# A hybrid decoder step on Trainium2: the FFN's down projection, 16 of 22 feature tiles as Strassen products

## The chip, the cores and the metric

One core of one Trainium2 chip runs the whole step as one program. The metric is the device time of the program in microseconds (us). For the kernel before there are three runs; their median is 1056.41 us.

## The reference, cut to what matters

One decoder layer for 512 prompt tokens and 8 sample tokens, width 1024, all in float32: token mixers, cross-attention, and last a SwiGLU feed-forward block of 2816 features.

```python
h = rms_norm(x, lp["g_ffn_pre"])
gt, up = jnp.split(h @ lp["w_gate_up"], 2, axis=-1)
f = (jax.nn.silu(gt) * up) @ lp["w_down"]
x = x + rms_norm(f, lp["g_ffn_post"])
```

`w_gate_up` is 1024 x 5632 and `w_down` is 2816 x 1024. Everything lies feature-major on the chip: a tile has 128 features on the partitions and the 520 tokens (8 sample, 512 prompt) along the free dimension. There are 8 tiles of width 1024 and 22 of 2816.

## The kernel before, in words

**Float32 by halves.** A matmul takes a value as two parts: `hi`, a rounding copy that ScalarE makes, and `lo`, the raw value less `hi`, a subtraction with two SBUF (or one PSUM and one SBUF) inputs on VectorE or GpSimd. A product of two float32 tiles is three matmuls: hi·hi, hi·lo, lo·hi. All of them move 256 to 264 token columns, one half of the 520 tokens, against a 128x128 weight.

**The front of the kernel** (input projection, RWKV scan, convolution, cross-attention) is not touched. At about 690 us the FFN's input `h` is made; its first 4 gate and 4 up tiles are done plainly (`dense`, L543, whose matmul is L556).

**Pairs as Strassen 2x2.** The other 18 gate and 18 up tiles are made in 18 units p, one gate and one up tile each (N_PAIRS = 18). The weight matrix of a unit is cut by gate/up and by first/last 4 tiles of `h`, the moving one by first/last 4 tiles and by LEFT/RIGHT 260 tokens. Seven products (`product`, L1806, matmul L1811) of 4 tiles x 3 matmuls, 84 matmuls, take the place of eight with 96. On TensorE unit p goes p6, p7, p2, p5, p1 of unit p+1, p4, p3. The four sums of operands of `h` (`t_raw`, `t_hi`, `t_lo`) are made once, ahead of the units, by operations over 1,040 columns.

**What the other engines do per unit.** VectorE, in this order (L3395 to L3510): `f_right` of the unit before (L3444), `gate_sums` (1,024 columns, two SBUF inputs, L3407), `second_sum` (L3414), `pair_f_low` of the unit before (L3448, 520 columns), `sum4_low` (L3434), `sum2_low` (L3429), y11 (L3492), `fourth_sum` (512 columns, two SBUF inputs, L3420), y22 (L3499), `sums13_low` (L3424), y21 (L3506), `f_left` (L3439). ScalarE makes the rounding copies (L2601, L2628), keeps three products (L2650, L2656, L2662), does the two silus (L2698, L2705) and `pair_f_high` (L2666). GpSimd makes three `lo` parts of 512 columns: up first half, gate second half, up second half (`pair_low`, L1055). p3 starts only when y22 has been read out of its bank, p7 of the next unit only when y21 has been used (before: by the left silu).

**The down projection** is plain: 8 output tiles m, each 22 feature tiles x 3 x 2 token halves, 132 matmuls, with weights in three blocks (8, 8 and 6 tiles, 24 blocks in all) that ScalarE (`split_hi`, L591) and GpSimd (`split_lo`, L1004) split. Six output tiles run through `dense`, the last two as pieces by token half (`down_piece`, L1878). ScalarE reads each output from PSUM twice, for its square and for the gained copy (`down_out`, L2718 and L2722), VectorE adds up the squares (`piece_add`, L3199).

**Queues.** All weight loads go through SyncE's queue in program order. `x_res`, the residual of 2,080 KB, was moved out to DRAM to make room; its return (L948) waits for the last product of the pairs, and stands between the fourth and the fifth load of down weights.

**The end.** When the first token half has all its squares, `half_sum` (L1168) and `half_root` give its norm, `half_add` (L3212, L3219) adds it to `x_res`, and `turn_tile` (L1888) transposes it for storing, while pieces of the second half fill TensorE. The last piece is followed by its squares, the root and the last transposes.

The order of work on every engine is written out by hand, with semaphores between the engines. Where two instructions of one engine follow, the later one can't pass the earlier.

## Time and profile before

| what | value |
|---|---|
| three runs, median (lowest, highest) | 1056.41 us (1055.25, 1056.93) |
| profiled execution, span of its instructions | 1055.9 us |
| TensorE busy | 1034.8 us, 98% |
| VectorE, ScalarE, GpSimd busy | 682.7, 517.8, 356.4 us |
| granted TensorE clock, mean | 0.999 |

The profile page gives no device time of its own for the profiled execution apart from the span, which lies 0.5 us under the median of the runs. The page's busy shares are means over the whole step. For this change the stretch from 735 us on counts: pairs to 916.5 us, down projection and end behind it.

### The profile page before, as it was taken

Reading aid. Unit: us, or ns where it says so; the run is one execution under the profiler, and the core shown is the slowest. Engines: PE = TensorE matmul, PEld = TensorE weight load, DVE = VectorE, ACT = ScalarE, POOL = GpSimd, SP = SyncE. Lnnn points to the kernel's source line nnn. Section 1 sums busy time; section 2 is a strip of 40 time slices with the busy share of each in tenths; the row PEclk is TensorE's granted clock in tenths of the full one; section 3 lists DMA queues with packets and bytes.
Section 4 is the critical chain, followed back from the end, with each engine's and each line's share of the span. In section 5 each row is a group of like instructions: output and inputs, shape, how many; then the busy total and the mean of one; then the engine's idle time right before and its main releaser. Section 6 shows DMA issues by size and latency. Waiting matters only on the chain.

```text
span 1055.9 us, 25943 instructions
## 1 busy us (share of the span) xinstructions
PE 1034.8 (98%) x10943; PEld 972.5 (92%) x10943; DVE 682.7 (65%) x1216; ACT 517.8 (49%) x967; POOL 356.4 (34%) x194
## 2 busy tenths in 40 slices
PE   8999999999999999999999999999999999999998
PEld 8998898998988998999999768989999999999998
DVE  5488888788785666786570791657998989500004
ACT  6455534544544567525462544654665665522232
POOL 4431221332312310256232101353544544444450
PEclk9999999999999999999999999999999999999999
DMA  7321221220223433655154774523334334433222
GB/s 228 100 70 35 61 62 43 61 76 27 62 62 102 130 102 130 209 180 164 57 200 160 259 276 131 147 76 105 110 92 120 105 97 121 161 115 100 81 64 82
DMA packets 164059, 120.41 MB, mean 114 GB/s; under 512 B 5336, under 2 KB 153066, under 8 KB 163433
## 3 DMA queue, kind: packets, MB, share of 16 engines
q1 hardware_dynamic: 159979, 108.08, 33.0%
q10 hardware_dynamic: 3974, 10.80, 2.9%
q8 instruction: 81, 1.33, 0.5%
q14 instruction: 25, 0.20, 0.1%
HBM read 111.04 MB, written 8.30 MB: 113 GB/s over the span
## 4 chain that ended last, share of the span: by engine, by line
PE 80%; DVE 13%; ACT 3%; DMA 2%; issue 2%; POOL 0%; DVEq 0%; ACTq 0%; SPq 0%
PE ps L556 34%; PE ps L1811 15%; PE ps L538 10%; PE ps L1168 10%; DVE conv_y L2859 5%; PE ps L1878 3%; PE ps L578 2%; DVE cache L3301 1%; DMA q_bc<-q_scratch 1%; PE ps L1115 1%; DVE ps L3214 1%; PE ps L604 0%; DMA w_raw<-in_w_gate_up_dram 0%; DMA x_tok<-in_x_prompt_dram 0%; DVE m_lo L640 0%
## 5 line engine op out<-in xcount | busy, mean ns | idle before, releaser
L1004 POOL TENSOR_TENSOR w_lo<-w_raw,w_hi 128x1024 fp32r<-128x1024 f32 (+2 forms) x83 | 193.7, 2338 | 408.7 <-ACT w_hi L596 356.5
L556 PE MATMUL ps<-h_hi,w_hi 128*128 128x260 f32 x748 | 161.8, 297 | 1.1 <-DVE gate_b L3156 0.5
L556 PE MATMUL ps<-h_hi,w_lo 128*128 128x260 f32 x748 | 150.2, 282 | 0.0
L556 PE MATMUL ps<-h_lo,w_hi 128*128 128x260 f32 x748 | 150.2, 282 | 0.0
L596 ACT ACTIVATE w_hi<-w_raw 128x1024 fp32r<-128x1024 f32 (+2 forms) x95 | 91.2, 965 | 74.0 <-PE ps L556 62.1
L556 PEld LDWEIGHTS ps<-h_hi,w_hi 128*128 128x128 f32 x748 | 115.3, 188 | 10.5 <-issue 4.4
L556 PEld LDWEIGHTS ps<-h_lo,w_hi 128*128 128x128 f32 x748 | 115.2, 188 | 0.0
L556 PEld LDWEIGHTS ps<-h_hi,w_lo 128*128 128x128 f32 x748 | 115.2, 188 | 0.0
L2859 DVE SCALAR_TENSOR_TENSOR conv_y<-glu,prm,conv_y 128x512 f32<-128x512 f32 x120 | 106.6, 889 | 2.5
L3199 DVE TENSOR_TENSOR sq_acc<-sq_acc,sq_tmp 128x264 f32<-128x264 f32 (+2 forms) x35 | 28.6, 816 | 114.8 <-ACT sq_tmp L2718 76.0
L1055 POOL TENSOR_TENSOR w_lo<-w_raw,w_hi 128x512 fp32r<-128x512 f32 x36 | 50.5, 1403 | 98.7 <-ACT w_hi L2601 98.7
L1168 PE MATMUL ps<-big 64*64 64x64 f32 (+1 forms) x1664 | 58.1, 232 | 5.5 <-ACT big L2053 3.6
L1004 POOL TENSOR_TENSOR wx_lo<-w_raw,wx_hi 128x1024 fp32r<-128x1024 f32 x12 | 28.7, 2394 | 101.5 <-ACT wx_hi L596 101.5
L1168 PEld LDWEIGHTS ps<-big 64*64 64x64 f32 x1664 | 48.4, 134 | 12.2 <-DVE tmp L2880 3.6
L556 PE MATMUL ps<-f_hi,w_hi 128*128 128x260 f32 x264 | 53.2, 283 | 0.3 <-DVE ps L3439 0.3
L556 PE MATMUL ps<-f_lo,w_hi 128*128 128x260 f32 x264 | 53.1, 283 | 0.0
L556 PE MATMUL ps<-f_hi,w_lo 128*128 128x260 f32 x264 | 53.1, 283 | 0.0
L556 PEld LDWEIGHTS ps<-f_hi,w_hi 128*128 128x128 f32 x264 | 40.7, 188 | 0.5 <-issue 0.5
L1811 PE MATMUL ps<-t_lo,w_hi 128*128 128x260 f32 x144 | 40.8, 283 | 0.0
L1811 PE MATMUL ps<-h_lo,w_hi 128*128 128x260 f32 x144 | 40.7, 283 | 0.0
L556 PEld LDWEIGHTS ps<-f_hi,w_lo 128*128 128x128 f32 x264 | 40.7, 188 | 0.0
L1811 PE MATMUL ps<-h_hi,w_hi 128*128 128x260 f32 x144 | 40.6, 282 | 0.0
(574 smaller groups left out, 3087.1 us busy)
## 6 DMA issues: line engine op xcount, KB each, us to landing
w_raw<-in_w_gate_up_dram SPq DMA_DIRECT2D x44, 512.0 KB, 4.7
w_raw<-in_w_in_dram SPq DMA_DIRECT2D x38, 512.0 KB, 3.7
cache<-in_cache_mem_k_dram SPq DMA_DIRECT2D x16, 512.0 KB, 6.3
w_raw<-in_w_down_dram SPq DMA_DIRECT2D x16, 512.0 KB, 3.7
cache<-in_cache_mem_v_dram SPq DMA_DIRECT2D x14, 512.0 KB, 7.3
w_raw<-in_w_k_dram SPq DMA_DIRECT2D x8, 512.0 KB, 3.9
w_raw<-in_w_v_dram SPq DMA_DIRECT2D x8, 512.0 KB, 3.6
w_raw<-in_w_out_dram SPq DMA_DIRECT2D x8, 512.0 KB, 3.7
```

Source lines behind the costliest of these rows:

```text
L538: mm = nc.tensor.matmul(ps[:, 2 * (b % 2) + h, 0:TOK_N[t][h]], w[:, k, :], x[:, k, TOK[t][h]], start=(k == 0 and n == 0), stop=(k == KT - ...
L556: mm = nc.tensor.matmul(ps[:, 2 * s + a, 0:width], w[:, k, :], x[:, x0 + k, a * width:(a + 1) * width], start=(first and k == 0 and n == 0 ...
L578: mm = nc.tensor.matmul(ps[:, 2 * a + m, :], x[:, k, P * m:P * (m + 1)], wide_rows(w)[:, kk, :], start=(k == 0 and n == 0), stop=(k == KT ...
L596: nc.scalar.activation(weights(b)[0][:, 0:kts], w_raw[:, b % RAW_SLOTS, 0:kts], ACT.Copy).then_inc(w_hi_ready, 1)
L1004: pool.tensor_tensor(lo[:, 0:kts], w_raw[:, b % RAW_SLOTS, 0:kts], hi[:, 0:kts].bitcast(F32), ALU.subtract).then_inc(w_lo_ready, 1)
L1055: pool.tensor_tensor(lo, raw, hi.bitcast(F32), ALU.subtract).then_inc(pair_lo, 1)
L1115: nc.tensor.matmul(ps[:, 2 * b + h, 0:EARLY_N[h]], hi[:, k, :], x[:, k, EARLY[h]], start=(k == 0 and n == 0), stop=False)
L1168: return nc.tensor.matmul(out, lhsT, rhs, start=start, stop=stop)
L1811: mm = nc.tensor.matmul(out, w[:, k, :], x[:, k, :], start=(start and k == 0 and n == 0), stop=(k == KT // 2 - 1 and n == 2), skip_group_c ...
L1878: mm = nc.tensor.matmul(ps[:, 2 * (m % 2) + h, 0:TOK_N[2][h]], w[:, k, :], x[:, k0 + k, TOK[2][h]], start=(j == 0 and k == 0 and n == 0), ...
L2859: link_v(stt(conv_y[:, p, 0:T], src, w, conv_y[:, p, 0:T], ALU.mult, ALU.add))
L3199: ins = tt(sq_acc[:, cols], sq_acc[:, cols], sq_tmp[:, n % 2, cols], ALU.add)
```

## The change

Eight units are put behind the 18 pairs (N_UNITS = 26). A down unit works on two output tiles (2q+1 and 2q, the place of gate and up) and on 8 of the first 16 feature tiles, as the same seven products; units 18 to 21 take feature tiles 0 to 7, units 22 to 25 tiles 8 to 15 and add to the results of 18 to 21 in `y_buf` in SBUF. The last 6 feature tiles (16 to 21) stay plain: 16 pieces of 18 matmuls, first all eight outputs of the first token half, then of the second, each added to `y_buf` by VectorE (`down_sum`).

The moving operands of the down units are parts of f named L, R, A, B, C, D (four tiles by 260 tokens, 1,040 columns): A, B, C, D are sums. f tiles 0 to 15 are now kept raw in SBUF as they come, and the sums, rounding copies and low parts of the parts are put into the loops by tables: `F_SUMS`, `F_LOWS` and their `_LATE` forms on VectorE, `F_HIGHS` on ScalarE, `FX_LOW_P` on GpSimd. Each such operation has 1,040 columns with SBUF inputs. `pair_f_high` and `pair_f_low` stay for f tiles 16 to 21 alone. In the down units f_left, f_right and the silus fall away; y11, y22, y21 go to `y_buf`, in units 22 to 25 as two operations each. The eight weight blocks of the last 6 feature tiles get storage of their own, seven of them in the room of used f parts. The return of `x_res` waits for the last product of all 26 units and again stands between the fourth and fifth load of the remaining blocks.

The diff, cut to its core:

```diff
-PAIR_BLOCKS = 2 * N_PAIRS
-N_BLOCKS = B_DOWN + 3 * KT
-DOWN_KT = (8, 8, 6)
+N_DOWN = 8
+N_UNITS = N_PAIRS + N_DOWN
+PAIR_BLOCKS = 2 * N_UNITS
+N_BLOCKS = B_DOWN + KT
+REST = 2 * KT
+REST_KT = FT - REST
...
+        if B_DOWN <= b < B_DOWN + 5:
+            return wd_a[:, b - B_DOWN], wd_b[:, b - B_DOWN]
+        if B_DOWN + 5 <= b < B_DOWN + 7:
+            return wd_b[:, b - B_DOWN], wd_b[:, b - B_DOWN + 2]
+        if b == B_DOWN + 7:
+            return w_hi[:, 0], w_lo[:, 0]
...
+    FX_HI = ("L0", "A0", "L1", "B0", "C0", "D0", "R1", "L2", "L3", "A2", "B2", "C2", "R3", "D2")
+    FX_LOW_V = ("L0", "B0", "C0", "L1", "A0", "D0", "C2", "B2", "D2")
+    FX_LOW_P = ("R1", "L2", "A2", "L3", "R3")
+    FX_RAW = ("A0", "B0", "C0", "D0", "A2", "B2", "C2", "D2")
...
+    FX_AT = {"L0": (rows(f_hi, 0, LEFT), rows(f_lo, 0, LEFT), rows(f_raw, 0, LEFT)),
+             "R0": (None, None, rows(f_raw, 0, RIGHT)),
+             "B0": (rows(f_hi, 0, RIGHT), rows(f_lo, 0, RIGHT), rows(f_raw, 0, RIGHT)),
+             "L1": (rows(f_hi, 1, LEFT), rows(f_lo, 1, LEFT), rows(f_raw, 1, LEFT)),
+             "R1": (rows(t_lo, 1, RIGHT), rows(f_lo, 1, RIGHT), rows(f_raw, 1, RIGHT)),
+             "A0": (rows(f_lo, 2, RIGHT), rows(f_lo, 2, LEFT), rows(f_raw, 2, LEFT)),
+             "C0": (rows(f_lo, 3, RIGHT), rows(f_lo, 3, LEFT), rows(f_raw, 3, LEFT)),
+             "D0": (rows(t_lo, 0, RIGHT), rows(f_hi, 1, RIGHT), rows(fh_raw, 1, RIGHT)),
+             "L2": (rows(h_hi, 0, LEFT), rows(f_hi, 2, LEFT), rows(fh_raw, 2, LEFT)),
+             "R2": (None, None, rows(fh_raw, 2, RIGHT)),
+             "B2": (rows(h_hi, 1, RIGHT), rows(f_hi, 2, RIGHT), rows(fh_raw, 2, RIGHT)),
+             "L3": (rows(t_lo, 1, LEFT), rows(f_hi, 3, LEFT), rows(fh_raw, 3, LEFT)),
+             "R3": (rows(t_lo, 0, LEFT), rows(f_hi, 3, RIGHT), rows(fh_raw, 3, RIGHT)),
+             "A2": (rows(h_hi, 1, LEFT), rows(h_lo, 0, LEFT), rows(hl_raw, 0, LEFT)),
+             "C2": (rows(h_lo, 1, RIGHT), rows(h_lo, 1, LEFT), rows(hl_raw, 1, LEFT)),
+             "D2": (rows(t_lo, 0, RIGHT), None, None)}
+    D2_LOW = (two(dx_low_a[:, :]), two(dx_low_b[:, :]))
+    D2_RAW = (two(rs[:, :]), two(silu[:, :]))
...
+    def f_operand(p, name):
+        g = 2 * ((p - N_PAIRS) // 4)
+        n = {"p1": f"L{g}", "p2": f"L{g + 1}", "p3": f"R{g + 1}", "p4": f"D{g}", "p5": f"A{g}", "p6": f"C{g}",
+             "p7": f"B{g}"}[name]
+        return n
...
+    def down_bank(m, h):
+        return (1, 3, 7, 1, 3, 7, 3, 1)[m] if h else (0, 2)[m % 2]
...
+            for m in range(KT):
+                src = weight_view("w_down")[:, REST:FT, P * m:P * (m + 1)]
+                if m < RAW_SLOTS:
+                    at = (B_DOWN + m) % RAW_SLOTS
+                    if m % 2 == 0:
+                        pair_slots_free(N_UNITS + m // 2)
+                    sp.dma_start(w_raw[:, at, 0:REST_KT], src).then_inc(w_landed[at], 16)
                 else:
-                    load(B_DOWN + n, src, kts=kts)
-                if n == RAW_SLOTS - 1:
+                    load(B_DOWN + m, src, kts=REST_KT)
+                if m == RAW_SLOTS - 1:
                     sp.wait_ge(product_done, PRODUCTS)
                     sp.wait_ge(x_moved, 16)
                     sp.dma_start(x_res[:, :, :].rearrange("p k n -> p (k n)"), x_scratch).then_inc(x_moved, 16)
...
+            def f_part_low(n):
+                hi, lo, raw = FX_AT[n]
+                pool.wait_ge(f_hi_ready, f_high(n))
+                pool.wait_ge(f_sums_made, f_summed({"R1": "D0", "L2": "A2", "A2": "C2", "L3": "D2", "R3": "D2"}[n]))
+                pool.tensor_tensor(lo, raw, hi.bitcast(F32), ALU.subtract).then_inc(f_low_p, 1)
+            for p in range(N_UNITS):
+                if p + 1 < N_UNITS:
                     pair_low(p + 1, "p1", pair_raw(p + 1)[2], "ua")
                 pair_low(p, "p4", pair_raw(p)[1], "gb")
-                if p + 1 < N_PAIRS:
+                if p == N_PAIRS:
+                    f_part_low("R1")
+                if p + 1 < N_UNITS:
                     pair_low(p + 1, "p2", pair_raw(p + 1)[3], "ub")
+                if N_PAIRS + 1 <= p < N_PAIRS + 5:
+                    f_part_low(FX_LOW_P[p - N_PAIRS])
...
+                if p in (N_PAIRS, N_PAIRS + 4):
+                    pe.wait_ge(*f_low(f_operand(p, name)))
...
+            def down_piece(m, h):
+                b = B_DOWN + m
                 hi, lo = weights(b)
                 pe.wait_ge(w_lo_ready, b + 1)
-                if j == 0 and h == 0:
-                    pe.wait_ge(out_taken[m % 2], (B_DOWN + m) // 2)
-                k0 = sum(DOWN_KT[:j])
-                for k in range(DOWN_KT[j]):
+                if h == 0 and m < 2:
+                    pe.wait_ge(f_made, fs(N_UNITS - 2 + m, 2))
+                elif h == 0:
+                    pe.wait_ge(down_summed, down_sums(m - 2, 0))
+                elif m < 2:
+                    pe.wait_ge(y_made, ys(N_UNITS - 1, ("y11", "y21")[m]))
+                elif m > 2:
+                    pe.wait_ge(down_summed, down_sums(m - 2 if m == 6 else m - 3, 1))
+                for k in range(REST_KT):
                     for n, (w, x) in enumerate(((hi, f_hi), (hi, f_lo), (lo, f_hi))):
-                        mm = nc.tensor.matmul(ps[:, 2 * (m % 2) + h, 0:TOK_N[2][h]], w[:, k, :], x[:, k0 + k, TOK[2][h]],
-                                              start=(j == 0 and k == 0 and n == 0),
-                                              stop=(j == 2 and k == DOWN_KT[2] - 1 and n == 2))
-                if j == 2:
-                    mm.then_inc(block_done if h else a_done, 1)
+                        mm = nc.tensor.matmul(ps[:, down_bank(m, h), 0:TOK_N[2][h]], w[:, k, :], x[:, REST + k, TOK[2][h]],
+                                              start=(k == 0 and n == 0), stop=(k == REST_KT - 1 and n == 2))
+                mm.then_inc(block_done if h else a_done, 1)
...
+            for m in range(KT):
+                down_piece(m, 0)
+            down_piece(0, 1)
             half_sum(2, 0)
-            down_piece(KT - 2, 1, 1)
-            down_piece(KT - 2, 2, 1)
-            down_piece(KT - 1, 0, 1)
-            pe.wait_ge(a_taken, A_TAKEN + 2)
+            for m in range(1, 5):
+                down_piece(m, 1)
+            pe.wait_ge(a_taken, A_TAKEN + KT)
             turn_tile(0, (0, 2), ready=KT * 4)
...
+            F_HIGHS = {1: ("L0",), 2: ("A0",), 5: ("L1",), 6: ("B0",), 7: ("C0",), 18: ("D0",), 19: ("L3",), 20: ("A2", "B2"),
+                       21: ("C2",), 22: ("D2",)}
+            F_HIGHS_LATE = {18: ("R1", "L2"), 21: ("R3",)}
+            def copy_up_right(p):
+                act.wait_ge(product_done, done(p, "p3"))
+                go(out_rows(p)[0][:, RIGHT], chain_bank(p), ACT.Copy).then_inc(f_made, 1)
...
+                if SPLIT_FROM < p <= N_PAIRS:
                     pair_f_high(p - 1)
+                if N_PAIRS < p <= N_PAIRS + 4:
+                    copy_up_right(p - 1)
+                for n in F_HIGHS.get(p, ()):
+                    f_part_high(n)
                 sum4_high(p)
                 keep_seventh(p)
+                for n in F_HIGHS_LATE.get(p, ()):
+                    f_part_high(n)
                 if more:
...
+                act.wait_ge(down_summed, down_sums(m, h))
...
+                rows = y_buf[:, m, TOK[2][h]]
+                go(sq_tmp[:, n % 2, TOK[2][h]], rows, ACT.Square).then_inc(post_squares, 1)
+                go(rows, rows, ACT.Copy, scale=prm_col("g_ffn_post", m)).then_inc(out_taken[m % 2] if h else a_taken, 1)
+            for b in range(B_DOWN + 2, B_DOWN + 4):
                 split_hi(b)
-            down_out(KT - 2, 0)
-            down_out(KT - 1, 0)
+            for m in range(KT):
+                if m == 3:
+                    act.wait_ge(product_done, PRODUCTS)
+                if m < 4:
+                    split_hi(B_DOWN + 4 + m)
+                down_out(m, 0)
+            down_out(0, 1)
             half_root(4)
...
+            def f_part_sum(n):
+                g = int(n[1])
+                raw = {m: FX_AT[m + str(i)][2] for m, i in (("L", g), ("R", g))}
+                left, right = FX_AT[f"L{g + 1}"][2], FX_AT[f"R{g + 1}"][2]
+                if n[0] == "A":
+                    if g:
+                        dve.wait_ge(product_done, done(N_PAIRS - 1, "p3"))
+                        dve.wait_ge(f_made, fs(REST - 5, 2))
+                    else:
+                        dve.wait_ge(out_taken[1], B_UP // 2 + 4)
+                    tt(FX_AT[n][2], raw["L"], raw["R"], ALU.subtract).then_inc(f_sums_made, 1)
+                    return
+                if n == "B0":
+                    dve.wait_ge(f_made, fs(KT - 5, 2))
+                dve.wait_ge(f_sums_made, f_summed(n) - 1)
+                if n[0] == "B":
+                    tt(FX_AT[n][2], raw["R"], right, ALU.subtract).then_inc(f_sums_made, 1)
+                elif n[0] == "C":
+                    stt(FX_AT[n][2], FX_AT[f"A{g}"][2], -1.0, right, ALU.mult, ALU.subtract).then_inc(f_sums_made, 1)
+                elif n == "D0":
+                    tt(FX_AT[n][2], left, FX_AT["C0"][2], ALU.add).then_inc(f_sums_made, 1)
+                else:
+                    for r in range(2):
+                        ins = tt(D2_RAW[r], left[:, 2 * r:2 * r + 2], FX_AT["C2"][2][:, 2 * r:2 * r + 2], ALU.add)
+                    ins.then_inc(f_sums_made, 1)
+            def f_part_low(n):
+                hi, lo, raw = FX_AT[n]
+                dve.wait_ge(f_hi_ready, f_high(n))
+                if n == "D2":
+                    for r in range(2):
+                        ins = tt(D2_LOW[r], D2_RAW[r], hi[:, 2 * r:2 * r + 2].bitcast(F32), ALU.subtract)
+                else:
+                    ins = tt(lo, raw, hi.bitcast(F32), ALU.subtract)
+                ins.then_inc(f_lo_ready, 1)
+            F_SUMS = {1: "A0", 4: "B0", 5: "C0", 6: "D0", 19: "A2", 20: "C2"}
+            F_SUMS_LATE = {19: "B2", 20: "D2"}
+            F_LOWS = {2: "L0", 7: "B0", 8: "C0", 9: "L1", 10: "A0", 18: "D0", 21: "C2", 22: "D2"}
+            F_LOWS_LATE = {21: "B2"}
...
+            def down_y(p, n):
+                up, gate = out_rows(p)
+                dst, bank, kept_part, op = {"y11": (up[:, LEFT], y11_bank, p1_kept_t[:, :], ALU.add),
+                                            "y22": (gate[:, RIGHT], chain_bank(p), p7_kept_t[:, :], ALU.subtract),
+                                            "y21": (gate[:, LEFT], y21_bank, n2_kept_t[:, :], ALU.subtract)}[n]
+                a, b = (kept_part, bank) if n == "y22" else (bank, kept_part)
+                if p < N_PAIRS + 4:
+                    tt(dst, a, b, op).then_inc(y_made, 1)
+                else:
+                    link_v(tt(kept_part, a, b, op))
+                    tt(dst, dst, kept_part, ALU.add).then_inc(y_made, 1)
+            def down_up_right(p):
+                dve.wait_ge(product_done, done(p, "p3"))
+                dst = out_rows(p)[0][:, RIGHT]
+                dve.wait_ge(f_made, fs(p - 4, 2))
+                tt(dst, dst, chain_bank(p), ALU.add).then_inc(f_made, 1)
+            for p in range(N_UNITS):
+                more = p + 1 < N_UNITS
+                if 0 < p <= N_PAIRS:
                     f_right(p - 1)
+                elif p > N_PAIRS + 4:
+                    down_up_right(p - 1)
                 if more:
                     gate_sums(p + 1)
                     second_sum(p + 1)
-                if p:
+                if SPLIT_FROM < p <= N_PAIRS:
                     pair_f_low(p - 1)
+                if p in F_SUMS:
+                    f_part_sum(F_SUMS[p])
+                if p in F_LOWS:
+                    f_part_low(F_LOWS[p])
...
+                if p in F_SUMS_LATE:
+                    f_part_sum(F_SUMS_LATE[p])
+                if p in F_LOWS_LATE:
+                    f_part_low(F_LOWS_LATE[p])
                 dve.wait_ge(product_done, done(p, "p4"))
                 dve.wait_ge(kept, keeps(p, "n2"))
-                tt(y21_bank, y21_bank, n2_kept_t[:, :], ALU.subtract).then_inc(y_made, 1)
-                f_left(p)
-                if p == 0:
-                    f_low(3)
-            f_right(N_PAIRS - 1)
-            pair_f_low(N_PAIRS - 1)
...
+            def down_sum(m, h):
+                dve.wait_ge(*((block_done, B_DOWN + m + 1) if h else (a_done, A_DONE + m + 1)))
+                if m == 0 and h == 0:
+                    dve.wait_ge(y_made, ys(N_UNITS - 1, "y21"))
+                    dve.wait_ge(f_made, fs(N_UNITS - 1, 2))
+                rows = y_buf[:, m, TOK[2][h]]
+                tt(rows, rows, ps[:, down_bank(m, h), 0:TOK_N[2][h]], ALU.add).then_inc(down_summed, 1)
+            for m in range(KT):
+                down_sum(m, 0)
+                if m:
+                    piece_add(2, m - 1, 0)
+            piece_add(2, KT - 1, 0)
+            down_sum(0, 1)
+            dve.wait_ge(a_taken, A_TAKEN + KT)
             dve.wait_ge(x_moved, 32)
-            half_add(4, range(KT), None)
-            piece_add(2, KT - 2, 1)
+            for m in range(4):
+                half_add(4, range(2 * m, 2 * m + 2), None)
+                down_sum(m + 1, 1)
+                piece_add(2, m, 1)
             dve.wait_ge(w_lo_ready, N_BLOCKS)
             dve.wait_ge(y_turns, 2)
             for d in range(2):
                 V.tensor_copy(y_tok(1)[:, 4 * P * d:4 * P * (d + 1)], ps[:, 4 + d, :]).then_inc(y_turn_v, 1)
```

## Rows read from the trace of the kernel before

**Rows 1.** The page, busy time of each engine (us, share, instructions).
```profile
PE 1034.8 (98%) x10943; PEld 972.5 (92%) x10943; DVE 682.7 (65%) x1216; ACT 517.8 (49%) x967; POOL 356.4 (34%) x194
```

**Rows 2.** Windows: window, length, busy us of PE, PEld, DVE, ACT, POOL; clock, DMA, GB/s.
```profile
800.00:900.00 100.00, 100.00 (x838) 100.00 (x837) 91.00 (x120) 60.52 (x120) 47.61 (x31) 1.00 0.36 106
...
950.00:1000.00 50.00, 50.00 (x419) 50.00 (x419) 2.38 (x4) 13.21 (x17) 21.22 (x10) 1.00 0.32 94
```

**Rows 3.** Timeline (start, us, instruction), TensorE, first matmul of two following pairs.
```profile
837.48 0.28 PE L1811 MATMUL ps<-t_hi,h_hi 128*128 128x260 f32 x1
...
847.54 0.28 PE L1811 MATMUL ps<-t_hi,h_hi 128*128 128x260 f32 x1
```

**Rows 4.** Timeline, VectorE, through one pair.
```profile
842.87 1.65 DVE L3420 TENSOR_TENSOR sum_tmp<-sum_tmp,w_raw 128x512 f32<-128x512 f32 x1
844.45 0.42 DVE L3499 TENSOR_TENSOR ps<-p_kept_t,ps 128x260 f32<-128x260 f32 x1
844.79 1.21 DVE L3424 TENSOR_TENSOR w_lo<-ps,w_hi 128x1024 fp32r<-128x1024 f32 x1
846.31 0.44 DVE L3506 TENSOR_TENSOR ps<-ps,n_kept_t 128x260 f32<-128x260 f32 x1 [0.32 <-PE ps L1811]
847.20 0.44 DVE L3439 TENSOR_TENSOR ps<-ps,silu 128x260 f32<-128x260 f32 x1 [0.45 <-ACT silu L2705]
...
848.09 2.05 DVE L3407 TENSOR_TENSOR ps<-w_raw 128x1024 f32<-128x1024 f32 x1
...
851.39 0.68 DVE L3434 TENSOR_TENSOR h_lo<-sum_tmp,h_hi 128x512 fp32r<-128x512 f32 x1
851.99 0.69 DVE L3429 TENSOR_TENSOR h_lo<-sum_tmp,h_hi 128x512 fp32r<-128x512 f32 x1
852.59 0.43 DVE L3492 TENSOR_TENSOR ps<-ps,p_kept_t 128x260 f32<-128x260 f32 x1
```

**Rows 5.** Timeline, GpSimd, the same pair.
```profile
842.69 1.29 POOL L1055 TENSOR_TENSOR w_lo<-w_raw,w_hi 128x512 fp32r<-128x512 f32 x1 [1.45 <-ACT w_hi L2601]
847.77 1.29 POOL L1055 TENSOR_TENSOR w_lo<-w_raw,w_hi 128x512 fp32r<-128x512 f32 x1 [3.79 <-ACT w_hi L2601]
849.01 2.28 POOL L1055 TENSOR_TENSOR zg_lo<-w_raw,zg_hi 128x512 fp32r<-128x512 f32 x1
```

**Rows 6.** Timeline, ScalarE, the same pair.
```profile
841.99 0.63 ACT L2601 ACTIVATE w_hi<-w_raw 128x512 fp32r<-128x512 f32 x1 [0.51 <-PE ps L1811]
...
846.78 0.39 ACT L2705 ACTIVATE silu<-ps 128x260 f32<-128x260 f32 x1 [1.21 <-DVE ps L3506]
847.07 0.62 ACT L2601 ACTIVATE w_hi<-w_raw 128x512 fp32r<-128x512 f32 x1
```

**Rows 7.** Timeline, operations of 1,024 to 1,040 columns between SBUF tiles, ahead of the pairs.
```profile
721.49 1.24 DVE L3461 TENSOR_TENSOR t_raw<-t_raw 128x1040 f32<-128x1040 f32 x1
...
721.21 3.95 ACT L2597 ACTIVATE t_hi<-t_raw 128x1040 fp32r<-128x1040 f32 x4
...
713.32 2.40 POOL L1004 TENSOR_TENSOR w_lo<-w_raw,w_hi 128x1024 fp32r<-128x1024 f32 x1
```

**Rows 8.** Timeline of SyncE behind the last product; DMA issues there, with time to landing.
```profile
916.71 0.34 SPq L948 DMA_DIRECT2D x_res<-x_scratch  x1
...
w_raw<-in_w_down_dram SPq DMA_DIRECT2D x1, 512.0 KB, 8.8
```

**Rows 9.** Timeline, ScalarE and GpSimd, the halves of one six-tile weight block.
```profile
1002.29 0.85 ACT L596 ACTIVATE w_hi<-w_raw 128x768 fp32r<-128x768 f32 x1 [3.67 <-PE ps L556]
...
1003.21 1.85 POOL L1004 TENSOR_TENSOR w_lo<-w_raw,w_hi 128x768 fp32r<-128x768 f32 x1 [2.12 <-ACT w_hi L596]
```

**Rows 10.** Timeline, TensorE and VectorE, around the first norm half of the end.
```profile
1030.96 0.61 PE L1168 MATMUL ps<-sq_acc,model_mean 128*128 128x264 f32 x2
...
1039.22 1.04 PE L1888 MATMUL ps<-ident,x_res 128*128 128x128 f32 x8
...
1038.04 0.42 DVE L3199 TENSOR_TENSOR sq_acc<-sq_acc,sq_tmp 128x256 f32<-128x256 f32 x1
```

276 lines of the change are left out of this document (147 added, 129 removed).

## The prediction, made before the changed kernel ran

> **What bounds the kernel now.** I read the page first: TensorE is busy 1034.8 of 1055.9 us [rows 1]. Then the windows from the pairs on [rows 2]: in the pairs TensorE is busy 100.00 of 100 us with VectorE at 91.00 and GpSimd at 47.61; in the down projection TensorE is full again and VectorE has 2.38 of 50 us. So matmuls set the time in both, but with very different cover: a pair has hardly 1 us of free VectorE, the plain down projection has nearly all of it. Last I read one pair engine by engine [rows 3 to 6], to find how late each result is. A change that takes matmuls out of the idle-VectorE stretch and turns that stretch into something like pairs saves TensorE time and spends VectorE's.
>
> **What goes.** The plain down projection has 8 x 132 = 1,056 matmuls. After: 8 units x 84 = 672, and 16 pieces x 18 = 288, in all 960. A pair lasts 847.54 - 837.48 = 10.06 us for 84 matmuls [rows 3], 0.1198 us each. 96 x 0.1198 = **-11.5 us**. The weight traffic is the same (8 units x 2 blocks of 512 KB, then 8 of 384 KB, for 16 and 8 before). ScalarE's reads of outputs in PSUM become reads in SBUF behind an addition on VectorE; in the 16 pieces that costs VectorE two operations of about 0.4 us in 2.16 us, beside TensorE. These are covered.
>
> **The lock between VectorE and GpSimd.** `fourth_sum` reads two SBUF tiles, has 512 columns as `sum4_low` has, and takes 1.65 us where that takes 0.68 [rows 4]: it begins at 842.87, GpSimd runs 842.69 to 843.98 [rows 5], and 843.98 + 0.54 is where it ends. `gate_sums` takes 2.05: GpSimd runs to 849.06, then 1.08 us. And GpSimd's next takes 2.28 for 1.29, since `gate_sums` held it up to 850.14. So such operations exclude each other whole, and whoever waits gets the next turn. The Trainium skill (SBUF — State Buffer, Who interferes with whom) says that the first to start holds the pair and the other fully blocks, which this agrees with; the same page gives about 115 ns more at a handover, and by that figure the forecast would be some 4 us later (five handovers a unit in seven units). The rows show 1.15 us of run behind a handover, under the 1.29 of a free one, so I add nothing.
>
> **Units 1 to 10.** `pair_f_low`, which reads PSUM and is free of the lock, falls away here; in units 1, 2 and 4 to 10 an operation of 1,040 columns with two SBUF inputs stands in its place, 1.24 us [rows 7], spacing 1.16. y22 ends at 844.87 [rows 4], TensorE wants it for p3 at 837.48 + 6 x 1.437 = 846.10: 1.2 us of slack. The first such unit uses it up: the operation waits for GpSimd until 851.29 (0.5), takes 1.1 instead of 0.6, and pushes `sum2_low` behind GpSimd's third low part (released by the copy at p2's end, 4.5 us into a unit [rows 6]), 1.2 more; `fourth_sum` then finds the lock free, 1.0 back. When the next unit is one too, everything hangs in a ring from one y22's end to the next: sums13_low 1.13, y21 0.44, silu 0.43, copy of up's first half 0.91, GpSimd 1.33, gate_sums 1.08, GpSimd 1.15, the new operation 1.10, GpSimd 1.15, sum4_low 0.54, sum2_low 0.61, y11 0.33, fourth_sum 0.61, y22 0.42, less 0.5 of overlapped starts: 10.7 us where the pace is 10.06. That is 0.62 per unit in units 5 to 10, 3.7, and 0.4 in unit 2: **+4.1 us**. Bounds: 0, if the third low part comes late enough to fall behind `fourth_sum`; 8, if both low parts and the sums collide each time.
>
> **Units 18 to 22.** Here the silus, f_left and f_right are gone (0.44 each on VectorE), but nearly all the operations on parts come together. Each is counted by what p3 or p7 waits for.
> - Unit 18: ScalarE does D0, R1 and L2 (0.99 each, [rows 7]) ahead of the copy that `sum2_low` needs, which ends 6.9 us into the unit; GpSimd's R1 low (2.4, [rows 7]) holds the lock to 8.0, sum2_low 0.54, GpSimd's waiting low part 1.15, fourth_sum 0.54, y22 0.4: 10.6 against 8.6. +2.0.
> - Unit 19: A2's sum, without f_right and silus: 0. Unit 20: C2's sum and two more copies of 0.99: y22 about 0.3 late. +0.3.
> - Unit 21: D2's sum (two halves) stands before y21 of unit 20, behind GpSimd's A2 low of 2.4: from y22's end, A2 low until 2.05, half 0.54, GpSimd 1.15, half 0.54, y21 0.4, in all 4.7; p7 is due at 2.9. +1.8.
> - Unit 22: y21 of unit 21 behind L3 low and B2 low, by the same count 3.5 against 2.9: +0.6. Then from y21's end a chain of lock turns: GpSimd 1.15, gate_sums 1.1, GpSimd 1.15, D2 low in halves 1.2, GpSimd 1.15, sum4_low 0.54, R3 low 2.4, sum2_low 0.55, y11 in two operations 0.8, fourth_sum 0.6, y22 in two 0.85: 11.5, which puts y22 at 13.6 in a unit where p3 is due at 9.4: +4.2.
> - Units 23 to 25 have the doubled adds but no parts: VectorE's 7.4 us and some 2 of lock fit: 0.
>
> Together **+8.9 us**. Bounds: 2 (only unit 18's ScalarE queue counts, the rest falls between) and 14 (each further collision another 1.2 in five units).
>
> **The last 6 tiles.** `x_res` goes out 0.2 us behind the last product; the fifth weight block stands behind it on SyncE's queue, and the one there now lands 8.8 us after its issue at 917.1 [rows 8]. Before, its place in the order was (132 + 48) x 0.1198 = 21.6 us on; now the fifth piece is due 4 x 18 x 0.1198 = 8.6 us after the last product. It lands at about 9.1 (384 KB for 512), then 0.85 on ScalarE and 1.85 on GpSimd [rows 9]: ready at 11.9. +3.3. Behind the blocked ScalarE the first square waits, behind that `piece_add` on VectorE and the next `down_sum`, which frees a bank; `piece_add` has two SBUF inputs and meets GpSimd's splits: +0.7. Between the half's `half_sum` and its transposes TensorE had 8.26 us of filler, and VectorE was done 1.2 us early [rows 10]; now VectorE has four `down_sum` and `piece_add` in between (3 us) against 8.6 us of filler: +0.5. The last piece's square has a `down_sum` and its release (0.42 + 0.2) in front: +0.6. **+5.1 us**, bounds 3 and 7.
>
> **The sum.** -11.5 + 4.1 + 8.9 + 5.1 = +6.6. The trace's span is 1055.9 us, 0.5 under the median of the three runs; I put the sum on the median: **1063.0 us**. A measurement of this kernel can tell about 0.2%, 2.1 us, from no change.
>
> **The rivals.**
> - *Likeliest, 0.59: the lock ring and the crowded units cost more than the matmuls give.* 1063.0, own range 1058.6 to 1071. For it: 91 of 100 us of VectorE and rows that show the lock. Against: the counts of units 20 to 22 build on each other.
> - *Faster, 0.31: the collisions mostly fall into gaps.* The new operations meet the lock free, as `sum4_low` does now; units 1 to 10 cost 0, the crowded ones 2, the end stays 5.1: -4.4, 1052.0. For it: the total of lock holders in such a unit is 7.7 of 10.06 us. It decides from where the stalls in the units are under 11.5 - 5.1 - 2.1 = 4.3. With the end hidden too, 1047.
> - *Even, 0.10: the two cancel*, stalls of 4.3 to 8.5 us in the units: 1056.4.
> - That the change doesn't do what it says would show as a count of matmuls other than 96 fewer; the loops in the diff leave no room for that, and I give it no chance of its own.
>
> The range: 1049 leaves out the case with the end hidden and part of the faster one, about 1 in 10; 1070 leaves out the upper bounds taken together, another 1 in 10. Chances: faster by over 0.2% 0.31, within 0.10, slower 0.59.
>
> **What the profile after would show.** 96 fewer TensorE instructions. Units 5 to 10 spaced 10.7 us instead of 10.06, with TensorE idle before p3, released by VectorE's y22; `fourth_sum` at 0.7 and `sum2_low` at 1.8 us there. Gaps before p3 of units 18 and 22 and before p7 of 21. A gap of about 3 us before the fifth piece, released by GpSimd's split of a block that landed late. Wrong: pairs still at 10.06 with the new operations in (the ring is looser than counted), or the fifth block ready in time.

## The result, and the profile after

The changed kernel takes **1069.46 us** (median of 4) against 1056.66 us of the kernel before on the same chip: ratio **1.0122**, 95% interval 1.0106 to 1.0138. That is 12.8 us slower, and the forecast 1063.0 us is 6.3 above the same median: the loss is twice the one forecast. All ratios compare runs in the faster of two states, and the medians of c5_later and c6_fill count one slower run each. The profiled execution has a span of 1067.1 us, 11.2 more than before.

The page after, to be set beside [rows 1]:

```profile
PE 1032.0 (97%) x10847; PEld 967.7 (91%) x10847; DVE 785.1 (74%) x1329; ACT 548.4 (51%) x1038; POOL 372.2 (35%) x207
```

TensorE has 96 instructions fewer (10,847 for 10,943), as the change says, and VectorE 113 more. But its busy time fell only by 2.8 us, where 96 matmuls are 11.5: some of the others must have become longer, by 8.7 us together. That is the first sign of what the forecast lacks.

The front of the kernel is the same in both, but in the two profiled executions it didn't last equally long. TensorE's first matmul of the pairs, before and then after:

```profile
735.07 0.28 PE L1811 MATMUL ps<-h_hi,w_hi 128*128 128x260 f32 x1
```

```profile
732.75 0.28 PE L1924 MATMUL ps<-h_hi,w_hi 128*128 128x260 f32 x1
```

So the front was 2.3 us shorter in the second, by chance, and from there to the end it is 320.8 us before and 334.3 us after: **+13.5 us**, and not 11.2, is what this pair of traces has to explain. Below, "from the pairs on" is reckoned in this way.

Whom TensorE waited for, from the pairs on (producer, total us, times, longest one). Before, the same view of that stretch has a single line of 0.3 us.

```profile
PE ps L1924 <- DVE y_buf L3661: 4.7, 2, 3.5
PE ps L1992 <- DVE y_buf L3728: 4.5, 1, 4.5
PE ps L1924 <- DVE ps L3701: 4.1, 8, 1.2
PE ps L1924 <- issue: 1.8, 1, 1.8
PE ps L1924 <- DVE y_buf L3658: 1.3, 1, 1.3
PE ps L1278 <- ACT sq_tmp L2853: 0.4, 1, 0.4
```

L3701 is y22 of a pair, L3658 and L3661 are single and doubled additions of a down unit, L3728 is `down_sum`. The long ones, in the timeline of TensorE (start, length, instruction, in brackets the idle time before it and who ended it):

```profile
754.20 0.36 PE L1924 MATMUL ps<-h_hi 128*128 128x260 f32 x1 [1.17 <-DVE ps L3701]
...
932.20 0.35 PE L1924 MATMUL ps<-t_lo,h_hi 128*128 128x260 f32 x1 [1.85 <-issue]
958.33 0.36 PE L1924 MATMUL ps<-f_hi,w_hi 128*128 128x260 f32 x1 [1.34 <-DVE y_buf L3658]
979.62 0.35 PE L1924 MATMUL ps<-t_lo,h_hi 128*128 128x260 f32 x1 [3.49 <-DVE y_buf L3661]
1011.37 0.36 PE L1924 MATMUL ps<-t_lo,h_hi 128*128 128x260 f32 x1 [1.16 <-DVE y_buf L3661]
1026.25 0.56 PE L1992 MATMUL ps<-f_hi,wd_a 128*128 128x264 f32 x1 [4.48 <-DVE y_buf L3728]
```

The bracket is the time in which no matmul runs. A matmul lasts 0.28 us and the next one otherwise begins 0.12 us after it, so a stall puts off all that follows by 0.16 us more than its bracket.

In order: unit 2's p3 (the first of eight such, 4.1 us together), unit 18's p3, unit 21's p7, unit 22's p3, unit 25's p3 and the third piece of the last tiles. All but unit 25's were forecast, the last one for the fifth piece. The waits add up to 16.8 us in 14 stalls, where before has three of 0.5 us together (two of them too short for that view), and the 0.16 of eleven more stalls makes 1.8. With the 11.5 us that went, that makes +6.6, and the traces have +13.5. **Some 7 us are in no wait.** Most of them are in the clock. Windows (start:end, length, busy us and instructions of PE, PEld, DVE, ACT, POOL; granted clock, DMA share, GB/s) around four of the stalls:

```profile
925.00:935.00 10.00, 8.15 (x59) 7.98 (x58) 8.93 (x10) 6.25 (x11) 7.17 (x5) 0.88 0.37 107
935.00:945.00 10.00, 10.00 (x82) 10.00 (x81) 8.04 (x10) 6.08 (x11) 4.55 (x3) 0.95 0.36 105
955.00:965.00 10.00, 8.65 (x72) 8.48 (x71) 9.97 (x11) 6.72 (x13) 6.20 (x5) 1.00 0.37 107
975.00:985.00 10.00, 6.51 (x42) 6.33 (x41) 9.26 (x12) 2.13 (x5) 4.48 (x3) 0.83 0.33 98
1025.00:1035.00 10.00, 8.75 (x52) 8.78 (x53) 6.61 (x9) 5.57 (x13) 6.41 (x4) 0.67 0.01 3
```

A full window of 10 us shows 84 to 86 matmuls. Behind unit 18's stall and behind unit 22's, TensorE is busy 8.15 and 6.51 us but issues 59 and 42 matmuls where 68 and 54 would fit; at the third piece 52 in 8.75 us. The granted clock is 0.88, 0.83 and 0.67 there. Microsecond by microsecond it is 0.50 (the 1.2 GHz level) from 933 to 936, from 981 to 983 and from 1025 to 1031, and 1.00 on either side of the first two. Behind unit 21's stall of 1.34 us it stays at 1.00. What was lost can be read from the windows: 10 us at 0.88 and 10 at 0.95 lack 1.7 us of full clock, 10 at 0.83 another 1.7, and the last window 3.3, of which 0.6 fell into the stall itself. Together that is **6.1 us** (0.8 us stay unexplained). The profiled execution is no odd one: the mean granted clock of the four runs is 0.991 to 0.995, against 0.999 before.

### The profile page after: what moved, and what is told of

Same layout as the page of the kernel before. It is cut to its first block, busy times and chain, and to the rows that moved or that the text cites. A ratio compares the mean times of both kernels' runs of the same rounds, so it can differ in the third digit from the quotient of the medians.

```text
span 1067.1 us, 26110 instructions
## 1 busy us (share of the span) xinstructions
PE 1032.0 (97%) x10847; PEld 967.7 (91%) x10847; DVE 785.1 (74%) x1329; ACT 548.4 (51%) x1038; POOL 372.2 (35%) x207
## 3 DMA queue, kind: packets, MB, share of 16 engines
q8 instruction: 84, 1.38, 0.5%
## 4 chain that ended last, share of the span: by engine, by line
PE 70%; DVE 20%; issue 4%; ACT 3%; DMA 2%; DVEq 0%; POOL 0%; ACTq 0%; SPq 0%; POOLq 0%
PE ps L570 25%; PE ps L1924 15%; PE ps L1278 10%; PE ps L552 10%; DVE conv_y L2989 4%; PE ps L1992 3%; PE ps L592 2%; DVE ps L3532 2%; DVE h_lo L3559 1%; DVE w_lo L3549 1%; DVE cache L3431 1%; DMA w_raw<-in_w_down_dram 1%; PE ps L1225 1%; DVE ps L3344 1%; DVE sum_tmp L3545 1%
## 5 line engine op out<-in xcount | busy, mean ns | idle before, releaser
L1103 POOL TENSOR_TENSOR w_lo<-w_raw,w_hi 128x1024 fp32r<-128x1024 f32 (+1 forms) x64 | 151.4, 2370 | 351.5 <-ACT w_hi L610 299.3
L570 PE MATMUL ps<-h_hi,w_hi 128*128 128x260 f32 x748 | 161.9, 298 | 0.8 <-DVE gate_b L3286 0.5
L570 PE MATMUL ps<-h_hi,w_lo 128*128 128x260 f32 x748 | 150.4, 282 | 0.0
L570 PE MATMUL ps<-h_lo,w_hi 128*128 128x260 f32 x748 | 150.4, 283 | 0.0
L1154 POOL TENSOR_TENSOR w_lo<-w_raw,w_hi 128x512 fp32r<-128x512 f32 x52 | 74.5, 1434 | 141.1 <-ACT w_hi L2709 141.1
L610 ACT ACTIVATE w_hi<-w_raw 128x1024 fp32r<-128x1024 f32 (+1 forms) x76 | 72.5, 958 | 25.9 <-PE ps L570 14.7
L1154 POOL TENSOR_TENSOR zg_lo<-w_raw,zg_hi 128x512 fp32r<-128x512 f32 x26 | 54.1, 2080 | 2.9 <-ACT zg_hi L2709 2.9
L1924 PE MATMUL ps<-h_hi,w_hi 128*128 128x260 f32 x192 | 54.4, 283 | 0.1
L1924 PE MATMUL ps<-h_hi,w_lo 128*128 128x260 f32 x192 | 54.2, 282 | 0.0
L3532 DVE TENSOR_TENSOR ps<-w_raw 128x1024 f32<-128x1024 f32 x26 | 51.5, 1981 | 0.0
L1924 PE MATMUL ps<-h_lo,w_hi 128*128 128x260 f32 x160 | 45.3, 283 | 0.0
L1924 PE MATMUL ps<-t_hi,w_lo 128*128 128x260 f32 x144 | 40.5, 282 | 0.0
L1924 PE MATMUL ps<-t_hi,w_hi 128*128 128x260 f32 x144 | 40.5, 281 | 0.0
```

The lines of the kernel that those rows point to most:

```text
L570: mm = nc.tensor.matmul(ps[:, 2 * s + a, 0:width], w[:, k, :], x[:, x0 + k, a * width:(a + 1) * width], start=(first and k == 0 and n == 0 ...
L610: nc.scalar.activation(weights(b)[0][:, 0:kts], w_raw[:, b % RAW_SLOTS, 0:kts], ACT.Copy).then_inc(w_hi_ready, 1)
L1103: pool.tensor_tensor(lo[:, 0:kts], w_raw[:, b % RAW_SLOTS, 0:kts], hi[:, 0:kts].bitcast(F32), ALU.subtract).then_inc(w_lo_ready, 1)
L1154: pool.tensor_tensor(lo, raw, hi.bitcast(F32), ALU.subtract).then_inc(pair_lo, 1)
L1924: mm = nc.tensor.matmul(out, w[:, k, :], x, start=(start and k == 0 and n == 0), stop=(k == KT // 2 - 1 and n == 2), skip_group_check=not ...
L3532: tt(sum_banks, two(others), quad(gate_a).unsqueeze(1).to_broadcast([P, 2, 4 * P]), ALU.add).then_inc(sums_made, 1)
```

## The experiments

**The slow clock by itself.** In `before`, three pairs get a hold of known length: ScalarE copies that rewrite two tiles of f_hi, which the results overwrite later, and p3 waits for them. Run d1_hold:

```diff
+    HOLD = {4: 2, 9: 3, 14: 5}
...
                 pe.wait_ge(y_made, ys(p, "y22"))
+                if p in HOLD:
+                    pe.wait_ge(held, list(HOLD).index(p) + 1)
                 product("p3", chain_bank(p), False)
...
+                if p in HOLD:
+                    for i in range(HOLD[p] - 1):
+                        link_a(go(f_hi[:, 20:22], h_hi[:, 0:2].bitcast(F32), ACT.Copy))
+                    go(f_hi[:, 20:22], h_hi[:, 0:2].bitcast(F32), ACT.Copy).then_inc(held, 1)
```

> The kernel before with three holds put in: in pairs 4, 9 and 14 TensorE waits before p3 for 2, 3 and 5 extra copies of 1,040 columns on ScalarE; results are unchanged. Expected stalls 1.3, 2.3 and 4.4 us. Theory (the clock falls behind a long enough stall): granted clock 1.00 behind the first, 0.5 for about 3.7 us behind the second and third, which costs about 1.9 us each: 8.0 of stalls and 3.8 of clock, 1068 us. Rival (stalls alone, the clock of the changed kernel fell for another reason): 1064.4 and a granted clock of 1.00 throughout.

Measured: 1068.57 us (one run), stalls of 1.23, 2.33 and 4.54 us, sum 8.1; +12.8 us from the pairs on (the span has only +10.7, since the front was 2.1 us shorter than in the trace of before). Run d2_hold is the same with other lengths:

> The kernel before, with TensorE held ahead of p3 in pairs 4, 14 and 9 by ScalarE copies that change nothing, sized between the earlier three holds: expected stalls about 1.8, 2.1 and 3.4 us (earlier 1.23, 2.33 and 4.54). Theory (behind a stall above some 2 us the clock falls, and the slow stretch has about one length, 3.5 to 4 us, however long the stall was): 1.00 behind the first, a fall behind the other two, span 1055.9 + 7.3 + 1.5 to 3.5 = 1065 to 1067. Rival (the loss grows with the stall): the 3.4 us hold loses more than half as much again as the 2.1 us one.

Measured: 1068.51 us (one run), stalls of 2.19, 3.44 and 2.12 us, sum 7.75; +12.6 from the pairs on. Windows behind the stalls of 1.23, 2.33 and 4.54, long enough to hold the whole slow stretch (d1_hold):

```profile
785.00:791.00 6.00, 5.92 (x49) 5.96 (x50) 4.57 (x7) 3.98 (x9) 3.54 (x2) 1.00 0.01 2
837.96:843.00 5.04, 5.04 (x29) 5.04 (x30) 2.94 (x4) 1.96 (x6) 2.51 (x2) 0.66 0.04 10
894.58:901.00 6.42, 6.42 (x33) 6.42 (x34) 2.91 (x4) 2.45 (x7) 2.52 (x2) 0.58 0.19 50
```

and behind 2.19, 3.44 and 2.12 (d2_hold):

```profile
786.00:791.00 5.00, 5.00 (x29) 5.00 (x30) 2.60 (x4) 1.91 (x6) 2.52 (x2) 0.66 0.02 5
841.52:849.00 7.48, 7.48 (x39) 7.48 (x40) 3.90 (x6) 3.14 (x8) 2.52 (x2) 0.59 0.34 99
896.95:903.00 6.05, 6.05 (x50) 6.05 (x51) 4.70 (x7) 3.94 (x10) 3.53 (x2) 1.00 0.02 4
```

Behind 1.23 and, in the other kernel, behind 2.12 the clock is 1.00 and some 50 matmuls fit into 6 us. Behind the other four the window lacks its length times what the clock lacks of 1.00: 1.7 us behind 2.33, 2.7 behind 4.54, 1.7 behind 2.19 and 3.1 behind 3.44. So a stall costs its own length, and a long one a slow stretch on top; for stalls near 2 us it can go either way, and the spread over all runs stands in the last section. The times bear the price out: from the pairs on, 12.8 - 8.1 - 0.5 (three times 0.16) leaves 4.2 us in d1_hold for slow stretches that lack 4.4, and 12.6 - 7.75 - 0.5 leaves 4.3 in d2_hold for 4.8. The rival of d2_hold (the loss grows with the stall) is half borne out: 3.1 behind 3.44 is well over one and a half times the 1.7 behind 2.19, but behind 4.54 it is only 2.7.

**The same in the changed kernel.** If the clock falls because TensorE stands still, matmuls that nothing reads must keep it up without ending any wait sooner. They take y11's bank, which is free until the next unit's p2. Run a6_fill:

```diff
+            def fill(n, bank):
+                for i in range(n):
+                    nc.tensor.matmul(bank, f_hi[:, REST, 0:P], f_hi[:, REST + 1, 0:HALF], start=True, stop=True)
...
                 product(p, "p4", y21_bank, False)
+                if p in (18, 22):
+                    pe.wait_ge(y_made, ys(p, "y11"))
+                    fill(13 if p == 18 else 27, y11_bank)
...
+                if m == 2:
+                    pe.wait_ge(y_made, ys(N_UNITS - 1, "y11"))
+                    fill(34, y11_bank)
                 down_piece(m, 0)
```

> The changed kernel, with matmuls that nothing reads put into its three longest stalls of TensorE: 13 ahead of p3 in unit 18 (stall 1.85 us), 27 ahead of p3 in unit 22 (3.49 us) and 34 ahead of the third piece of the last tiles (4.48 us), at 0.12 us each 1.56, 3.24 and 4.08 us, so that each ends before what TensorE waits for there. They take y11's bank, which is free by then. Nothing else is touched, and each wait ends when it did. Theory (the clock is lost because TensorE stood still): the granted clock stays 1.00 behind all three, the stalls show as 0.3 to 0.4 us each, and the 5 to 6 us that the sum of stalls and removed matmuls leaves open are gone: span 1061 to 1062.5, time 1063 to 1065. Rival 1 (the matmuls behind these places are slow because of what runs beside them on the other engines): still half speed there, time 1069 to 1070. Rival 2 (the stalls themselves are the whole price and the rest is scattered): 1069 to 1070 with the clock at 1.00.

Measured: 1067.80 us, ratio 1.0116 (1.0100 to 1.0132). The clock is 1.00 behind all three, but the time is above the 1063 to 1065 expected: a miss, with a plain cause in the trace. In unit 22 y11's addition had ended only 2.04 us into the stall, the 27 matmuls began then, and they ran on 2 us past y22. By its interval this run can't be told from the changed kernel. Run a7_fill cuts them to 11:

> The changed kernel with the unread matmuls of the run a6_fill, the 27 of unit 22 cut to 11. In a6_fill they could only start when y11's double addition was done, 2.04 us into the stall, and at 3.3 us they ran on past the end of the wait by some 2 us (y22 had landed at 978.91, they ended at 981.07); 11 take 1.3 us and end about when y22 lands. Theory (the clock is lost because TensorE stands still, and those 2 us of overrun are why a6_fill was only 1.7 us below the changed kernel): clock 1.00 behind all three stalls, span of the profiled execution 1061.5 to 1063, median time 1063.5 to 1066 (changed kernel 1069.5). Rival (a kept clock is worth 2 us at most): 1067 or more.

Measured: **1064.74 us**, ratio 1.0073 (1.0055 to 1.0091), span 1061.5. Waits and windows of a7_fill:

```profile
PE ps L1924 <- DVE ps L3711: 4.1, 8, 1.2
PE ps L1953 <- DVE y_buf L3671: 2.0, 1, 2.0
PE ps L1924 <- DVE y_buf L3668: 1.4, 1, 1.4
PE ps L1924 <- DVE y_buf L3671: 1.2, 1, 1.2
```

```profile
925.00:935.00 10.00, 9.85 (x81) 9.56 (x80) 8.94 (x11) 6.57 (x11) 7.79 (x5) 1.00 0.36 107
935.00:945.00 10.00, 10.00 (x86) 10.00 (x85) 9.45 (x12) 6.08 (x11) 5.59 (x3) 1.00 0.36 107
975.00:985.00 10.00, 7.96 (x65) 7.82 (x65) 9.71 (x15) 3.60 (x8) 3.46 (x3) 1.00 0.33 96
1025.00:1035.00 10.00, 10.00 (x84) 9.94 (x83) 6.49 (x11) 4.27 (x12) 3.11 (x2) 1.00 0.01 2
```

Clock 1.00 in every window where it was 0.88 to 0.67. Waits (9.1) and filler (58 x 0.12 = 7.0) together are 16.1 us, hardly less than the changed kernel's waits of 16.8 in the same stretch, and yet the median is 4.7 us lower, and the trace from the pairs on 6.0. So this is the term that no wait shows: **4 to 5.5 us for the clock**, where the windows of the changed kernel lack 6.1, and the rival (2 us at most) falls.

**The last tiles.** Run a1_xres_last sends the read of `x_res` behind all weight blocks on SyncE's queue, nothing else:

```diff
-                if m == RAW_SLOTS - 1:
+                if m == KT - 1:
                     sp.wait_ge(product_done, PRODUCTS)
```

> The changed kernel with one edit: the return of x_res is issued behind all eight remaining weight blocks instead of behind the fourth. Theory (a stall costs its own length and then some us of matmuls at half the clock): the gap of 4.48 us before the third piece goes and with it the stretch of 90 matmuls that took 13.49 instead of 10.78 us, together 7.2: 1069.5 to 1062.3 us. Rival 1 (only the wait counts, the slow clock has another cause): the gap goes, the slow stretch stays, 1065.0. Rival 2 (GpSimd's splits or the sums on VectorE bound the pieces anyway): under 2 us of gain, 1067.5 or more.

Measured: 1062.42 us, ratio 1.0057 (1.0040 to 1.0074): 7.0 us gained by one line, more than the stall of 4.5 that it removes, since the slow stretch goes with it (85 matmuls from 1025 to 1035 for 52). Part of the 7.0 isn't its own: unit 18's stall is there with 1.86 us, but in this execution no slow stretch followed it. The chain that it cuts, in the changed kernel (SyncE's issues, ScalarE's and GpSimd's splits, VectorE):

```profile
1013.09 0.34 SPq L1047 DMA_DIRECT2D x_res<-x_scratch  x1
1013.47 8.67 SPq L902 DMA_DIRECT2D w_raw<-in_w_down_dram  x4
1022.88 0.84 ACT L610 ACTIVATE wd_a<-w_raw 128x768 fp32r<-128x768 f32 x1 [12.22 <-DMA w_raw<-in_w_down_dram]
1023.80 1.80 POOL L1103 TENSOR_TENSOR wd_b<-w_raw,wd_a 128x768 fp32r<-128x768 f32 x1 [8.90 <-ACT wd_a L610]
1024.07 1.69 DVE L3326 COPY sq_acc<-sq_tmp 128x264 f32<-128x264 f32 x1 [6.20 <-ACT sq_tmp L2853]
1025.68 0.42 DVE L3728 TENSOR_TENSOR y_buf<-y_buf,ps 128x264 f32<-128x264 f32 x1
```

The block's issue at 1013.47 stands behind `x_res`, it lands 9.4 us later (8.8 in [rows 8], for a larger block), ScalarE's first half goes at 1022.88, the square that had queued behind it at 1023.63, and then `piece_add` takes 1.69 us: it ends at 1025.76, and GpSimd's split of the same block, begun before it, ends at 1025.60. This first `piece_add` is a copy with one SBUF input, so here too VectorE stood for GpSimd, though the operation hasn't the two inputs of which the forecast spoke. Only then comes `down_sum`, which frees the third piece's bank. The stall came at the third piece and not at the fifth, 4.48 us long for a forecast of 3.3 + 0.7.

**Units 1 to 10.** Run a2_parts_late moves their nine part operations behind `sums13_low`:

```diff
-            F_SUMS = {1: "A0", 4: "B0", 5: "C0", 6: "D0", 19: "A2", 20: "C2"}
-            F_SUMS_LATE = {19: "B2", 20: "D2"}
-            F_LOWS = {2: "L0", 7: "B0", 8: "C0", 9: "L1", 10: "A0", 18: "D0", 21: "C2", 22: "D2"}
-            F_LOWS_LATE = {21: "B2"}
+            F_SUMS = {19: "A2", 20: "C2"}
+            F_SUMS_LATE = {1: "A0", 4: "B0", 5: "C0", 6: "D0", 19: "B2", 20: "D2"}
+            F_LOWS = {18: "D0", 21: "C2", 22: "D2"}
+            F_LOWS_LATE = {2: "L0", 7: "B0", 8: "C0", 9: "L1", 10: "A0", 21: "B2"}
```

> The changed kernel with one edit: the nine operations of 1,040 columns of units 1 to 10 stand behind sums13_low instead of ahead of sum4_low, with the same work. Theory (the ring of turns at the lock with GpSimd): there the lock is free, p3 no longer waits for y22, and the eight stalls of 4.1 us in all fall under 1: 1066 us or less. Rival (VectorE has simply too much work in these units, wherever it stands): the stalls move to another product and stay at 3 to 4 us, 1069.

Measured: 1063.97 us, ratio 1.0063 (1.0046 to 1.0080); the eight stalls are gone from the waits, the others stand as they did (4.7, 4.5, 1.9 and 1.4). The median gained 5.5, the traces from the pairs on differ by 3.7: between them lie the 4.1 of the waits. The rival (the stalls move to another product) falls.

**Unit 18: ScalarE's queue or the lock?** The forecast's count has both: three copies on ScalarE, behind which the one that `sum2_low` needs ends 6.9 us into the unit, and GpSimd's R1 low, which holds the lock to 8.0. Run a3_unit18 takes one of them (L2's) to unit 19:

```diff
-F_HIGHS = {..., 19: ("L3",), ...}
-F_HIGHS_LATE = {18: ("R1", "L2"), 21: ("R3",)}
+F_HIGHS = {..., 19: ("L2", "L3"), ...}
+F_HIGHS_LATE = {18: ("R1",), 21: ("R3",)}
```

> The changed kernel with one edit: ScalarE's rounding copy of L2 goes from unit 18 to unit 19. Theory of the prediction (the queue of copies on ScalarE ahead of the one that sum2_low needs makes the stall of 1.85 us in unit 18): the stall falls to about 0.9 and the clock behind it stays at 1.00, 2.5 us in all, 1067. Rival (the turns at the lock alone make it, GpSimd's R1 low and the low part behind it): the stall stays at 1.85, and the time within 1 us of 1069.5.

Measured: 1072.16 us (one run); `sum2_low` begins earlier, but the stall stays at 1.84, and a new one of 2.18 stands at 957.22, where L2's copy now is in the way. Run c2_free joins this with the two remedies above and lets the second operations read and write banks free of the lock, as the next fence shows for y22:

```diff
-                    link_v(tt(kept_part, a, b, op))
-                    tt(dst, dst, kept_part, ALU.add).then_inc(y_made, 1)
+                    room = f_banks[:, 1] if n == "y22" else bank
+                    link_v(tt(room, a, b, op))
+                    tt(dst, dst, room, ALU.add).then_inc(y_made, 1)
```

> Both edits, and two more: ScalarE's copy of L2 goes from unit 18 to unit 19, and the second operation of y11, y22 and y21 in units 22 to 25 reads its first input from PSUM, so that it has no two SBUF inputs and needs no lock. Theory: against the changed kernel -7.2 (x_res), -3.5 (units 2 to 10), -2.9 (unit 18: stall from 1.85 to about 0.9 and no slow stretch behind it), -1.2 (unit 25), -0.8 (unit 22): 1054 us, a little under the kernel before. Rival (collisions only move): 1060 or more.

Measured: 1058.89 us, ratio 1.0019 (1.0006 to 1.0032), between the theory and its rival; the stall of unit 25 is gone, 1.85 still stand in unit 18 and 3.5 in unit 22, and 2.15 in unit 20, to which L2's copy moved. VectorE in unit 18 of the changed kernel (`gate_sums`, `sum2_low`, y22), then the same of c2_free with GpSimd's R1 low as its last line:

```profile
922.10 2.05 DVE L3532 TENSOR_TENSOR ps<-w_raw 128x1024 f32<-128x1024 f32 x1
928.31 1.78 DVE L3554 TENSOR_TENSOR h_lo<-sum_tmp,h_hi 128x512 fp32r<-128x512 f32 x1 [1.07 <-ACT h_hi L2709]
931.69 0.41 DVE L3658 TENSOR_TENSOR y_buf<-p_kept_t,ps 128x260 f32<-128x260 f32 x1
```

```profile
919.47 2.07 DVE L3532 TENSOR_TENSOR ps<-w_raw 128x1024 f32<-128x1024 f32 x1
924.72 2.74 DVE L3554 TENSOR_TENSOR h_lo<-sum_tmp,h_hi 128x512 fp32r<-128x512 f32 x1
929.07 0.41 DVE L3658 TENSOR_TENSOR y_buf<-p_kept_t,ps 128x260 f32<-128x260 f32 x1
924.25 2.66 POOL L1163 TENSOR_TENSOR f_lo<-f_raw,t_lo 128x1040 fp32r<-128x1040 f32 x1 [1.56 <-ACT t_lo L2802]
```

From `gate_sums` to y22 it is 931.69 - 922.10 = 9.59 us and 929.07 - 919.47 = 9.60. Without the ScalarE copy `sum2_low` (L3554) has no wait for it any more (1.07 before), but it meets GpSimd's R1 low and takes 2.74 us instead of 1.78. So L2's copy is not in the path of y22, and R1's low on GpSimd is. ScalarE isn't out of it altogether: R1's low itself waited 1.56 us for ScalarE's copy of R1 (last line), ahead of which D0's copy stands, and no run moved those two.

**Order in units 18 to 25.** Run a4_y22_first puts y11 and y22 ahead of `sum2_low` and `fourth_sum`, and the late part operations behind y21, in the down units only:

```diff
-                if more:
+                if more and p < N_PAIRS:
                     sum2_low(p + 1)
...
-                if more and p:
+                if more and p and p < N_PAIRS:
                     fourth_sum(p + 1)
...
+                if more and p >= N_PAIRS:
+                    sum2_low(p + 1)
+                    fourth_sum(p + 1)
                 if more:
                     sums13_low(p + 1)
```

> The changed kernel with one edit: in the down units VectorE takes y11 and y22 ahead of sum2_low and fourth_sum, and the late part operations behind y21, with the same work. Theory (p3 waits for a reader that needs no lock but stands in the queue behind two that do): stall of unit 18 from 1.85 to 0.3, of unit 21 from 1.34 to 0.3, of unit 22 from 3.5 to 0.8 (R3 low itself on GpSimd), and no slow clock behind any of them: 5.3 of stalls and about 4 of clock less, 1060.5 us. Rival (the lock has too little time in these units in whatever order): the stalls go to p6 and p7 of the next units, 1066 or more.

Measured: 1067.65 us, ratio 1.0111 (1.0085 to 1.0138): the rival. Unit 18's stall went, but 3.37 us (unit 22's p7 waits for B2's low), 0.70 and 2.04 us now stand in unit 22; the stalls from 733 us on add up to 17.8 us, for 16.8. That the time isn't longer has its cause in the clock: only the last of these stalls has a slow stretch behind it. Run c3_order joins the remedies of a1, a2 and the free banks with this order:

> The changed kernel with four edits: x_res behind all weight blocks, the parts of units 1 to 10 late, the lock-free second operations, and the order of VectorE in the down units (L2's copy stays in unit 18). By the sum of the single runs: 1069.5 - 7.1 (x_res, measured) - 5.5 (parts late, measured) - 1.2 (unit 25) - 9 (order) = 1046.7 us, about 1% under the kernel before. Rival (what is won in one unit is paid in the next): 1053 or more.

Measured: 1056.05 us, ratio 0.9997 (0.9983 to 1.0010): the time of the kernel before, and again the rival's. The order has gained something here: c2_free, which lacks it (and has L2's copy in unit 19), took 1058.89. Where it stalls, and a window of it:

```profile
951.92 0.36 PE L1924 MATMUL ps<-f_hi,w_hi 128*128 128x260 f32 x1 [1.38 <-DVE y_buf L3658]
965.60 0.36 PE L1924 MATMUL ps<-h_hi,w_hi 128*128 128x260 f32 x1 [3.40 <-DVE f_hi L3642]
```

```profile
943.00:967.00 24.00, 19.23 (x158) 18.87 (x158) 23.90 (x25) 13.86 (x26) 14.80 (x8) 1.00 0.33 96
```

From 943 to 967 VectorE is busy 23.90 of 24 us, against 91.00 of 100 in a pair [rows 2]. From one `gate_sums` to the next it takes 11.7 us (942.04, 953.76, 965.38), where TensorE's unit takes 10.06: VectorE has more work, with its waits for the lock, than fits. Run c5_later tests whether another place for the lock's holders helps. It takes GpSimd's L2 and A2 lows away from the fourth sums:

```diff
-                if p == N_PAIRS:
-                    f_part_low("R1")
+                if p in (N_PAIRS, N_PAIRS + 2, N_PAIRS + 3):
+                    f_part_low({N_PAIRS: "R1", N_PAIRS + 2: "L2", N_PAIRS + 3: "A2"}[p])
...
-                if N_PAIRS + 1 <= p < N_PAIRS + 5:
+                if N_PAIRS + 3 <= p < N_PAIRS + 5:
                     f_part_low(FX_LOW_P[p - N_PAIRS])
```

> The version with four remedies (x_res behind the last block, parts of units 1 to 10 late, lock-free second operations, y22 ahead of the sums in the down units; 1056.05), and on top GpSimd's part lows L2 and A2 put behind the next unit's p4 low, so that they no longer stand where VectorE makes the fourth sum (2.92 us there instead of 1.66). Theory (in units 19 to 21 VectorE is busy without a gap from 921 to 969 us, so it is the amount of work under the shared lock that counts, and a turn saved at one operation is taken at another): stalls of TensorE between 942 and 967 still add up to 4 to 5 us, time 1055 to 1057. Rival (the place of GpSimd's operations is what costs): the fourth sums fall to 1.7 us, stalls fall by about 2.4 us, time 1052 to 1053.5.

Measured: 1057.66 us, ratio 1.0012 (1.0001 to 1.0024), a little above the 1055 to 1057 expected and far from the rival's 1052 to 1053.5. VectorE in the same halves of D2's sum and the same fourth sum, c3_order, then c5_later:

```profile
947.36 2.94 DVE L3545 TENSOR_TENSOR sum_tmp<-sum_tmp,w_raw 128x512 f32<-128x512 f32 x1
953.15 0.69 DVE L3631 TENSOR_TENSOR silu<-fh_raw,hl_raw 128x520 f32<-128x520 f32 x1
```

```profile
948.16 0.68 DVE L3545 TENSOR_TENSOR sum_tmp<-sum_tmp,w_raw 128x512 f32<-128x512 f32 x1
951.72 2.94 DVE L3631 TENSOR_TENSOR silu<-fh_raw,hl_raw 128x520 f32<-128x520 f32 x1
```

The fourth sum fell from 2.94 to 0.68, as wished, and the half of D2's sum rose from 0.69 to 2.94: GpSimd's A2 low (951.20 to 954.11) now stands there. Stalls between 942 and 967: 0.99 + 4.21 = 5.2, against 1.38 + 3.40 = 4.8. Moving these two lows gained nothing, which is what the theory says: the amount of work under the lock counts, not its place.

**A version that beats both.** What can still be had in c3_order is the clock behind its 3.40 us. Run c6_fill adds 26 unread matmuls there:

```diff
                 product(p, "p6", chain_bank(p), False)
+                if p == 22:
+                    pe.wait_ge(y_made, ys(p - 1, "y11"))
+                    fill(26, y11_bank)
```

> The same version (1056.05), with 26 matmuls that nothing reads ahead of p7 in unit 22, where TensorE stands 3.40 us for B2's low and then runs about 3.3 us at half speed. Theory of the clock: no slow stretch, stall down to 0.3 us, 1.6 to 1.8 us gained: time 1054.0 to 1054.8, below the kernel before (1056.7) by 0.2%. Rival: no change, 1056.

Measured: **1054.60 us**, ratio to before **0.9983** (0.9972 to 0.9994), the clock 1.00 and 77 matmuls in the window of 10 us in which c3_order has 0.83 and 62:

```profile
965.00:975.00 10.00, 9.46 (x77) 9.31 (x78) 9.65 (x13) 4.53 (x8) 5.87 (x4) 1.00 0.36 107
```

The gain over c3_order, 1.45 us in the medians, is within the two intervals, but it fits the 1.7 us that the window lacks at 0.83. So the change can be made to pay, but by the ratio only some 1.8 us (0.6 to 3.0) of its 11.5, and only with four remedies and the filler.

## Why the prediction was wrong in size, and what of it held

- **-11.5, what goes**: right, 96 instructions.
- **+4.1, units 1 to 10**: right in kind and nearly in size, 4.1 in eight stalls (5.3 with the 0.16 of each), released by y22; without the operations they are gone (a2_parts_late). VectorE from one y22 to the next, units 7 to 8, the rows that answer to [rows 4]:

```profile
827.68 0.42 DVE L3701 TENSOR_TENSOR ps<-p_kept_t,ps 128x260 f32<-128x260 f32 x1
...
833.60 1.60 DVE L3642 TENSOR_TENSOR f_lo<-f_raw,f_hi 128x1040 fp32r<-128x1040 f32 x1
835.13 1.78 DVE L3559 TENSOR_TENSOR h_lo<-sum_tmp,h_hi 128x512 fp32r<-128x512 f32 x1
837.77 0.68 DVE L3545 TENSOR_TENSOR sum_tmp<-sum_tmp,w_raw 128x512 f32<-128x512 f32 x1
838.37 0.42 DVE L3701 TENSOR_TENSOR ps<-p_kept_t,ps 128x260 f32<-128x260 f32 x1
```

838.37 - 827.68 = 10.69 us, where the ring was counted as 10.7, and the fourth sum has 0.68 for 1.65. The turn is lost at `sum4_low` (L3559, 1.78), one operation earlier than forecast.
- **+8.9, units 18 to 22**: 7.8 in all. Unit 18 was 1.85 for 2.0, by the term of the count that ends at 8.0, R1's low on GpSimd against `sum2_low`; the copy ready at 6.9, and with it "unit 18's ScalarE queue" that the lower bound names, cost nothing by itself (a3_unit18, c2_free). Unit 20 cost nothing for 0.3, unit 21 1.34 for 1.8, unit 22 3.49 for 0.6 + 4.2. **Units 23 to 25 were set at 0, and unit 25 cost 1.16**: the second operation of the doubled additions has SBUF inputs and met GpSimd's splits (L3661); in free banks the stall is gone (c2_free). That the sum came within 1.1 us is in part luck: unit 22 was set 1.3 too high and unit 25 1.2 too low.
- **+5.1, the last tiles**: 4.48 for 3.3 + 0.7, at the third piece. From the `half_sum` to the end it is 27.5 us for 24.9 + 2.15 (one piece more), so 0.45 for 0.5 + 0.6.
- These sum to 4.1 + 7.8 + 4.9 - 11.5 = +5.3, close to the +6.6 forecast. **The step that failed is the sum itself**: it priced each stall at its own length and let the matmuls behind it run at 0.1198 us each, so the clock was a term put at nothing without a word. Three of the stalls, 1.85, 3.49 and 4.48 us long, were followed by stretches at 0.50 of the clock, which lack 6.1 us of full clock; with the clock kept at 1.00, a7_fill is 4.7 us faster by the median and 6.0 from the pairs on. A smaller term was missing too: 0.16 us a stall, 1.8 in all. From the pairs on: -11.5 + 16.3 of waits + 1.8 + 6.1 = 12.7, of 13.5.

The clock stood at 1.00 in the windows of before [rows 2] because TensorE never stood still there, so they could not show the price; the forecast took a stall's length for its whole cost without a bound for it. The Trainium skill (TensorE: Matmul & The Clock Gate, Part 1: The HAM clock gate) says that TensorE's clock follows how busy it has lately been and goes down to half when it idles. The rows agree: the granted clock is 1.00 or 0.50, and it fell behind stalls, or near the end of long ones, and, from the pairs on, never in a full stream.

That the two cancel, or that the collisions fall into gaps (the faster rival), is out: the stalls of the units alone are 11.9 us. The forecast's direction and the mechanisms that it named held, but 1069.46 lies only just under the range's end of 1070, and it came there by the clock, which no bound of the range had counted.

Open: why nearly equal stalls have a slow stretch behind them in one run and not in the next (1.85 in the changed kernel and in c2_free, 2.19 and 2.12 in d2_hold). No run here separates that. The GpSimd lows of units 18 to 22 could not be taken out by themselves, so that the amount of work under the lock sets the time there is argued from moving it (c5_later), not shown by removing it. And 0.8 us from the pairs on are in none of the terms.

## What to carry to other kernels

Price a stall of a busy TensorE in two terms: its length, and for a long one (here nearly every one of 2.3 us or more, and some near 2 us) another 1.7 to 3.1 us lost by matmuls at half clock behind it; so remove or fill the longest stall first, it pays more than its length. Before work is moved next to a VectorE that is 91% busy, add up what both VectorE and GpSimd must do under their lock per unit of TensorE's time: above that, a new order moves most of the stall to another place. When two traces are compared, take them from the first instruction that the change can reach, since an unchanged front varied by 2.3 us here. And when a stage becomes shorter, look at what its first late transfer stands behind; here one line on the queue was worth 7 us.

## What the runs showed of the hardware

- What follows a stall of TensorE from the pairs on, in all the profiled executions of this case (a slow stretch is one in which the granted clock is 0.50; a window of 1 us then shows 6 or 7 matmuls, and 10 or 11 at 1.00):

| stall, us | how many | slow stretch behind |
|---|---|---|
| 1.16 to 1.39 | 22 | none |
| 1.84 to 2.19 | 12 | 4 (three of 1.84 to 1.87, one of 2.19) |
| 2.33 to 4.54 | 15 | 14; not behind one of 3.37 (a4_y22_first) |

Many of these stalls are the same one in kernels that differ elsewhere, and two of the twelve stand in front of fillers. The stretch did not last in proportion: some 3.4 us behind 1.85, some 5.3 behind 4.48, some 6.1 behind 3.44 (d2_hold).
- It need not begin with the first matmul: behind the 3.40 us of c3_order the matmuls up to 966.89 start 0.12 to 0.13 us apart, after the first, and from there to 970.1 some 0.22 apart. Nor need it wait for the end of the stall: before the third piece the clock was 0.50 from 1025 on, and work began at 1026.25.
- The lock passes turn by turn even against a full queue: an operation of 0.68 us took 2.94 when it met one of GpSimd's 1,040 columns (1,024 columns take 2.4 us alone [rows 7]), and its neighbour 0.68 again (c5_later).
